# Unread unit-matrix matmuls in nine kinds ahead of the upward products, and half of the 512-token products as two halves

## The chip, the cores and the metric

The kernel runs on one core of one Trainium2 chip. The metric is the device time of one execution in microseconds (us), lower is better.

## The reference

Two transformer blocks of two layers each on 256 tokens of width 1024, in float32, and a context stream of 256 more tokens in the second block. Cut to the parts that carry the time:

```python
# first block, twice
mod = silu(c) @ w_ada[l] + b_ada[l]
h = rms_norm(x, g_pre_mix[l]) * (1 + sc_m) + sh_m
y = token_mixer(h, ...)                      # h @ w_in, two attentions, @ w_out
x = x + gt_m * rms_norm(y, g_post_mix[l])
h = rms_norm(x, g_pre_ffn[l]) * (1 + sc_f) + sh_f
y = (gelu(causal_conv3(h @ w_up_act)) * (h @ w_up_lin)) @ w_down     # 1024 -> 2816 -> 1024
x = x + gt_f * rms_norm(y, g_post_ffn[l])
# second block, on x and ctx; every FFN half is a SwiGLU 1024 -> 2816 -> 1024
s = s + 0.5 * gate * ((silu(h @ wg) * (h @ wu)) @ wd)
# layer 0: FFN half, convolution module (h @ w1, 31 taps, layer norm, @ w2), FFN half
# layer 1: FFN half, neighbourhood attention (h @ w_qkv, ..., @ w_o), FFN half on x alone
```

Only the x stream is returned.

## The kernel before, in words

A planner (`Plan`) writes out the whole program as one list of steps, and five classes, one per engine, walk that list and issue their own part of each step. Semaphores count finished work; `wait_ge` waits on such a count. So the order of the work on each engine is that of the list.

All weights come from DRAM in units of 128 x 1024 numbers, numbered in the order in which the planner takes them (`Plan.unit`). A ring of eight `raw` buffers receives them by SP's DMAs. ScalarE rounds a unit to fp32r (`upper`, line 1510, into `sh`), VectorE subtracts to get the remainder (`lower`, line 1806, into `sl`), in rings of six. Unit numbers also go to the modulation weights, which are not split and which VectorE alone multiplies (line 1820), between the others at planned rates. Activations are split in the same way into `hH` and `hL`, tokens along the columns: 256 for x alone, 512 with the context. A true product is then three fp32r matmuls that add in one PSUM bank, issued by `Tensor.mm3` at lines 1239 (high by high), 1240 (high weights by low activations in upward products) and 1241.

Upward products (step `prod`, method `Tensor.prod`) hold a 128 x 128 block of weights stationary and stream the tokens. One call works through one unit: eight blocks k, 24 matmuls, all of 256 or all of 512 columns, into one of eight PSUM banks. Its waits come first: that the bank is free, that the unit is split (`weights`), and ahead of each k that the activations are there (`act_ready`). Calls come from:

- `ffn1` (first block, each layer): 22 pairs of products of 256 tokens (`w_up_act`, `w_up_lin`), one stage of 44 calls each.
- `ffn2` on both streams (three times): the first three pairs go through `products`, in two passes of 256 tokens each over the same units (`begun` marks the second pass of each, which goes to the other half of the bank), so that the first can start before all tokens are normalized. Then 8 pairs of 512 tokens, the downward half, 11 pairs of 512 tokens, the downward half. Between the first products stand transposes (`turn`, line 1352) of the norm still under way.
- `ffn2` on x alone (the last): four pairs are made token by token, then 7 and 11 pairs of 256 tokens.
- `conv`: three pairs by `products`, five pairs of 512 tokens; the taps of the convolution (line 1447, plain f32) and the mean (line 1459) stand between them.
- `na`: eight products of 256 tokens for the queries, eight of 512 for the keys, with attention steps between.

Downward products (`down`) hold activations stationary and stream weights, 512 columns; they go through `mm3` as well.

Plain f32 work on TensorE is of other lines: transposes (1352, 1277, 1367, 1415: the data stationary, the unit matrix streamed, 128 columns), the attention's last matmul (1435, 64 columns), the taps (1447, 512 columns), and `warm` (line 1264), which issues matmuls of 256 columns with the unit matrix of the constants `C` as the stationary operand into a bank whose content nobody reads. `warm` stands ahead of stages at which TensorE would wait.

Of the kernel before, what the change touches and what calls it, by code (L numbers as in the profile page):

```python
# [16 lines left out]
KD = 8  # L17
# [33 lines left out]
for _n, _i, _w in VECS:  # L51
    VAT[(_n, _i)] = NV
    NV += _w

C_ID, C_0, C_CM, C_CS = 0, 128, 256, 384
NCST = 384 + 32

# [1165 lines left out]
class Tensor(Engine):  # L1223
# [79 lines left out]
    def prod(self, s):  # L1303
        cols = s["cols"]
        b = s["b"]
        if not s.get("begun"):
            self.wait_ge(self.gone(b))
        hi, lo = self.weights(s["unit"])
        H, L = self.m["hH"], self.m["hL"]
        w = cols.stop - cols.start  # L1310
        out = self.buf(b)[:, cols] if "begun" in s else self.buf(b)[:, 0:w]
        for k in range(KD):
            self.act_ready(s["act"], k, range(cols.start // 128, cols.stop // 128))
            c = slice(k * 128, (k + 1) * 128)
            x = self.mm3(out, hi[:, c], lo[:, c], H[:, k, cols], L[:, k, cols], k == 0, k == KD - 1)
        x.then_inc(self.sems["mm"], 1)
        if s["last"]:
            self.done("mm", ("full", b), ("w_used", s["unit"]), ("act_used", s["act"]))
        else:
            self.done("mm")  # L1320
# [1170 lines left out]
```

## Time and profile before

| what | us |
|---|---|
| median of the two runs shown | 2509.11 (2506.05 to 2512.16) |
| the profiled execution, its own time | 2495.19 |
| its span, first to last instruction | 2493.4 |
| PE (TensorE matmul) busy | 2411.0 of the span |
| PEld (TensorE weight load) busy | 2026.2 |
| DVE (VectorE) busy | 1677.2 |
| ACT (ScalarE) busy | 1082.1 |
| mean granted TensorE clock | 0.99 |

The profile is of one execution. Matmuls are pipelined: a duration of one is longer than the time to the start of the next, so what a stream of them costs is read from the starts, or from the length of a stretch over the matmuls in it. A granted clock of 1.00 is 2.4 GHz, 0.50 is 1.2 GHz. In a table of stretches the number in brackets counts every instruction that touches the stretch, so it can be one or two over the matmuls that start there.

### The profile page before, as it was taken

The page shows a single profiled execution, that of the slowest core. Times are in us where ns is not written, and L with a number is a line of the kernel's source. Part 1 is how long each engine was busy: PE and PEld are TensorE (multiplying, and loading weights), DVE is VectorE, ACT ScalarE, POOL GpSimd, SP SyncE. Part 2 cuts the span into 40 slices and gives each one's busy share as a digit, 9 for nine tenths or more (in the row PEclk, how much of TensorE's full clock was granted, in tenths as well). Part 3 has the DMA queues.
Part 4 walks back from the last instruction along what each step waited for, and adds up shares of the span by engine and source line. Part 5 has one row for each costly group of instructions (what it writes and reads, how often), then busy time and mean ns, then how long its engine had stood idle before and what let it go on. Part 6 is the DMA issues. An engine that isn't in the chain of part 4 may idle for free.

```text
span 2493.4 us, 34671 instructions
## 1 busy us (share of the span) xinstructions
PE 2411.0 (97%) x13076; PEld 2026.2 (81%) x13076; DVE 1677.2 (67%) x2620; ACT 1082.1 (43%) x1851; POOL 394.2 (16%) x431
## 2 busy tenths in 40 slices
PE   6999999989999999999979999999999999999998
PEld 5778987779988888887648888889888888777997
DVE  6967987769995776777965565565565556356554
ACT  4566545666554222237744322224322225344543
POOL 1111101101211101106840100100100110001101
PEclk9999999999999999999989999999999999999999
DMA  8656885557773454442202443442453443322562
GB/s 323 233 197 217 311 315 191 193 195 253 267 258 123 186 203 171 167 173 77 68 26 96 150 178 120 166 169 94 152 186 123 156 144 127 106 90 91 190 202 94
DMA packets 123335, 422.55 MB, mean 169 GB/s; under 512 B 15904, under 2 KB 20128, under 8 KB 123168
## 3 DMA queue, kind: packets, MB, share of 16 engines
q1 hardware_dynamic: 122608, 418.55, 48.1%
q8 instruction: 104, 1.70, 0.3%
q10 hardware_dynamic: 560, 1.79, 0.2%
q14 instruction: 63, 0.52, 0.1%
HBM read 419.17 MB, written 1.11 MB: 169 GB/s over the span
## 4 chain that ended last, share of the span: by engine, by line
PE 88%; DVE 6%; ACT 2%; issue 1%; POOL 1%; DMA 0%; DVEq 0%; ACTq 0%; POOLq 0%
PE ps L1239 27%; PE ps L1240 27%; PE ps L1241 27%; PE ps L1435 2%; PE ps L1447 2%; DVE sl L1806 1%; PE ps L1352 1%; DVE mjunk L1820 1%; PE ps L1415 1%; POOL ap L2335 1%; PE ps L1404 1%; ACT junk L1533 0%; DMA X<-in_x 0%; DVE sc L2021 0%; DVE hL L1895 0%
## 5 line engine op out<-in xcount | busy, mean ns | idle before, releaser
L1510 ACT ACTIVATE sh<-raw 128x1024 fp32r<-128x1024 f32 x534 | 552.2, 1043 | 898.8 <-PE ps L1241 898.3
L1239 PE MATMUL ps<-hH,sh 128*128 128x256 f32 (+1 forms) x2496 | 821.2, 329 | 1.6 <-DVE hL L1895 1.6
L1241 PE MATMUL ps<-hH,sl 128*128 128x256 f32 (+1 forms) x2496 | 816.5, 327 | 0.0
L1240 PE MATMUL ps<-hL,sh 128*128 128x256 f32 (+1 forms) x2496 | 816.5, 327 | 0.0
L1806 DVE TENSOR_TENSOR sl<-raw,sh 128x1024 fp32r<-128x1024 f32 x534 | 640.8, 1220 | 110.8 <-ACT sh L1510 110.2
L1820 DVE CUSTOM_DVE_ANT_0 mjunk<-raw,cB,V 128x1024 bf16<-128x1024 f32 x384 | 499.1, 1300 | 26.3 <-DMA C<-in_cst 8.6
L1239 PEld LDWEIGHTS ps<-hH,sh 128*128 128x128 f32 x2496 | 469.4, 188 | 52.9 <-issue 5.2
L1240 PEld LDWEIGHTS ps<-hL,sh 128*128 128x128 f32 x2496 | 468.7, 188 | 49.2 <-issue 1.7
L1241 PEld LDWEIGHTS ps<-hH,sl 128*128 128x128 f32 x2496 | 469.2, 188 | 48.1
L2308 POOL TENSOR_TENSOR uLl<-F,uHh 128x256 fp32r<-128x256 f32 (+1 forms) x132 | 170.8, 1294 | 1165.2 <-ACT uHh L1695 1043.0
L1241 PE MATMUL ps<-sh,uLl 128*128 128x512 f32 x792 | 311.8, 394 | 0.0
L1240 PE MATMUL ps<-sl,uHh 128*128 128x512 f32 x792 | 311.7, 394 | 0.0
L1239 PE MATMUL ps<-sh,uHh 128*128 128x512 f32 x792 | 310.5, 392 | 0.0
L2133 DVE TENSOR_TENSOR F<-S,ps 128x512 f32<-128x512 f32 (+1 forms) x88 | 54.6, 621 | 306.8 <-issue 283.7
L1239 PE MATMUL ps<-sh,hH 128*128 128x512 f32 (+2 forms) x512 | 204.5, 399 | 19.2 <-DVE hL L1895 9.7
L1240 PE MATMUL ps<-sl,hH 128*128 128x512 f32 (+2 forms) x512 | 197.2, 385 | 0.0
L1241 PE MATMUL ps<-sh,hL 128*128 128x512 f32 (+2 forms) x512 | 197.1, 385 | 0.0
L1239 PEld LDWEIGHTS ps<-sh,uHh 128*128 128x128 f32 x792 | 148.9, 188 | 33.8 <-DVE sl L1806 0.4
L1240 PEld LDWEIGHTS ps<-sl,uHh 128*128 128x128 f32 x792 | 149.0, 188 | 33.5
L1241 PEld LDWEIGHTS ps<-sh,uLl 128*128 128x128 f32 x792 | 149.0, 188 | 31.6
L1239 PEld LDWEIGHTS ps<-sh,hH 128*128 128x128 f32 x512 | 98.1, 192 | 41.9 <-issue 16.0
L1241 PEld LDWEIGHTS ps<-sh,hL 128*128 128x128 f32 x512 | 97.8, 191 | 19.7
(168 smaller groups left out, 2058.5 us busy)
## 6 DMA issues: line engine op xcount, KB each, us to landing
raw<-in_w SPq DMA_DIRECT2D x752, 512.0 KB, 4.6
G<-gates SPq DMA_DIRECT2D x14, 512.0 KB, 6.3
raw<-in_w SPq DMA_DIRECT2D x16, 256.0 KB, 4.6
cB<-in_rpb SPq DMA_DIRECT2D x64, 64.0 KB, 2.7
raw<-in_w SPq DMA_DIRECT2D x4, 492.0 KB, 6.1
S<-in_rows SPq DMA_DIRECT2D x6, 256.0 KB, 3.3
X<-in_x ACTq DMA_DIRECT2D x1, 1024.0 KB, 12.1
X<-in_ctx SPq DMA_DIRECT2D x1, 1024.0 KB, 5.8
```

The source lines that it names most:

```text
L1239: self.e.matmul(out, lh, rh, start=start, stop=False)
L1240: self.e.matmul(out, lh, rl, start=False, stop=False)
L1241: return self.e.matmul(out, ll, rh, start=False, stop=stop)
L1352: x = self.e.transpose(self.buf(p["b"])[:, k * 128:(k + 1) * 128], src[:, k * 128:(k + 1) * 128], ident)
L1404: x = self.e.matmul(ps[:, :], self.m["qT"][pr, c, i], self.m["kT"][pr, c, :], start=True, stop=True)
L1435: x = self.e.matmul(o[:, 64 * (hd % 8):64 * (hd % 8) + 64], p[:, (j * nb + c) * 128:(j * nb + c + 1) * 128], v, start=c == 0, stop=c == nb ...
L1447: x = self.e.matmul(ps[:, :], wd[:, k, :], up[:, :, k:k + 256], start=k == 0, stop=k == n - 1)
L1510: self.e.activation(self.m["sh"][k % SPL][:, 0:w], self.m["raw"][r % RAW][:, 0:w], ACT.Copy).then_inc(self.sems["w_hi"], 1)
L1806: self.e.tensor_tensor(lo[:, 0:w], raw[:, 0:w], hi[:, 0:w].bitcast(F32), ALU.subtract).then_inc(self.sems["w_lo"], 1)
L1820: self.e.tensor_tensor_reduce(out=self.m["mjunk"][:, :], in0=raw[:, 0:D], in1=self.m["cB"][:, st, :], scale=1.0, scalar=o, op0=ALU.mult, o ...
L2133: self.e.tensor_tensor(F[:, 0:N], self.buf(s["s"])[:, 0:N], self.buf(s["bu"])[:, s["o"]:s["o"] + N], ALU.mult).then_inc(self.sems["v_ps"], 1)
L2308: self.e.tensor_tensor(lo, self.buf(s["f"])[:, 0:N], hi.bitcast(F32), ALU.subtract).then_inc(self.sems["p_sb"], 1)
```

## The change

`Tensor.prod` gets a list of nine kinds, `NUDGES`, each a number of matmuls and a width. The kind is chosen by the weight unit, `unit // 2 % 9`. Ahead of the product's first true matmul so many matmuls with the unit matrix stationary and the first columns of the constants streamed are written into the same columns of the bank; the true product, which begins with `start=True`, overwrites them. In addition a product of 512 tokens whose unit number has `unit % 8 < 4` is made as two halves of 256 tokens, each through all eight k and each with its own unread matmuls. All other steps and their order stay.

```diff
--- before.py
+++ after.py
@@ -52,6 +52,7 @@
     VAT[(_n, _i)] = NV
     NV += _w
 
+NUDGES = ((0, 0), (1, 128), (2, 128), (1, 64), (1, 32), (1, 256), (2, 64), (1, 16), (1, 96))
 C_ID, C_0, C_CM, C_CS = 0, 128, 256, 384
 NCST = 384 + 32
 
@@ -1309,10 +1310,18 @@
         H, L = self.m["hH"], self.m["hL"]
         w = cols.stop - cols.start
         out = self.buf(b)[:, cols] if "begun" in s else self.buf(b)[:, 0:w]
-        for k in range(KD):
-            self.act_ready(s["act"], k, range(cols.start // 128, cols.stop // 128))
-            c = slice(k * 128, (k + 1) * 128)
-            x = self.mm3(out, hi[:, c], lo[:, c], H[:, k, cols], L[:, k, cols], k == 0, k == KD - 1)
+        halves = (slice(0, 256), slice(256, 512)) if w == 512 and s["unit"] % 8 < 4 else (slice(0, w),)
+        for half in halves:
+            n, wide = NUDGES[s["unit"] // 2 % len(NUDGES)]
+            part = slice(cols.start + half.start, cols.start + half.stop)
+            for k in range(KD):
+                self.act_ready(s["act"], k, range(part.start // 128, part.stop // 128))
+                if k == 0:
+                    for _ in range(n):
+                        self.e.matmul(out[:, half.start:half.start + wide], self.m["C"][:, C_ID:C_ID + 128],
+                                      self.m["C"][:, 0:wide], start=True, stop=True)
+                c = slice(k * 128, (k + 1) * 128)
+                x = self.mm3(out[:, half], hi[:, c], lo[:, c], H[:, k, part], L[:, k, part], k == 0, k == KD - 1)
         x.then_inc(self.sems["mm"], 1)
         if s["last"]:
             self.done("mm", ("full", b), ("w_used", s["unit"]), ("act_used", s["act"]))
```

## Rows read from the trace of the kernel before

**Rows 1.** The page: busy shares, and the chain that ended last by engine and line.
```profile
PE 2411.0 (97%) x13076; PEld 2026.2 (81%) x13076; DVE 1677.2 (67%) x2620; ACT 1082.1 (43%) x1851; POOL 394.2 (16%) x431
...
PE 88%; DVE 6%; ACT 2%; issue 1%; POOL 1%; DMA 0%; DVEq 0%; ACTq 0%; POOLq 0%
PE ps L1239 27%; PE ps L1240 27%; PE ps L1241 27%; PE ps L1435 2%; PE ps L1447 2%; DVE sl L1806 1%; PE ps L1352 1%; DVE mjunk L1820 1%; PE ps L1415 1%; POOL ap L2335 1%; PE ps L1404 1%; ACT junk L1533 0%; DMA X<-in_x 0%; DVE sc L2021 0%; DVE hL L1895 0%
```

**Rows 2.** Table of stretches, PE alone: start:end us, length, busy (matmuls), granted clock, DMA share, GB/s.
```profile
207.79:327.57 119.78, 119.78 (x1057) 1.00 0.83 294
559.65:679.44 119.79, 119.79 (x1057) 1.00 0.74 259
742.74:753.72 10.98, 10.98 (x100) 1.00 0.46 144
754.51:777.21 22.70, 22.70 (x196) 1.00 0.41 136
777.21:866.81 89.60, 89.60 (x387) 1.00 0.44 160
866.81:927.25 60.44, 60.44 (x266) 1.00 0.53 194
1116.30:1124.57 8.27, 8.27 (x76) 1.00 0.67 230
1125.36:1139.58 14.22, 14.22 (x124) 1.00 0.37 112
1378.40:1468.00 89.60, 89.60 (x386) 1.00 0.41 144
1468.00:1529.60 61.60, 61.60 (x266) 1.00 0.41 147
2327.28:2365.47 38.19, 38.19 (x339) 1.00 0.58 193
2395.69:2455.55 59.86, 59.86 (x529) 1.00 0.63 206
```

**Rows 3.** Timeline of PE: start us, duration us, engine, line, operation; behind the fourth upward product of an ffn2.
```profile
753.37 0.28 PE L1239 MATMUL ps<-hH,sh 128*128 128x256 f32 x1
753.49 0.28 PE L1240 MATMUL ps<-hL,sh 128*128 128x256 f32 x1
753.60 0.28 PE L1241 MATMUL ps<-hH,sl 128*128 128x256 f32 x1
753.72 1.03 PE L1352 MATMUL ps<-C,PT 128*128 128x128 f32 x8
754.51 0.36 PE L1239 MATMUL ps<-hH,sh 128*128 128x256 f32 x1
754.71 0.28 PE L1240 MATMUL ps<-hL,sh 128*128 128x256 f32 x1
754.83 0.28 PE L1241 MATMUL ps<-hH,sl 128*128 128x256 f32 x1
754.94 0.28 PE L1239 MATMUL ps<-hH,sh 128*128 128x256 f32 x1
755.06 0.28 PE L1240 MATMUL ps<-hL,sh 128*128 128x256 f32 x1
755.18 0.28 PE L1241 MATMUL ps<-hH,sl 128*128 128x256 f32 x1
```

**Rows 4.** Chain that ended last, in order of time: start us, us, group.
```profile
1186.57 5.16 PE ps L1447 x12
...
2168.60 0.84 PE ps L1435 x8
2295.32 0.87 PE ps L1352 x8
2296.20 6.05 PE ps L1264 x28
```

**Rows 5.** Timeline of PE around two transposes between downward matmuls of the second mixer.
```profile
504.23 0.39 PE L1241 MATMUL ps<-sh,hL 128*128 128x512 f32 x1
504.46 0.38 PE L1415 MATMUL ps<-C,S 128*128 128x128 f32 x2
504.60 0.48 PE L1239 MATMUL ps<-sh,hH 128*128 128x512 f32 x1
504.91 0.39 PE L1240 MATMUL ps<-sl,hH 128*128 128x512 f32 x1
505.14 0.40 PE L1241 MATMUL ps<-sh,hL 128*128 128x512 f32 x1
505.37 0.40 PE L1239 MATMUL ps<-sh,hH 128*128 128x512 f32 x1
```

**Rows 6.** Table of stretches, all engines: busy us (instructions) of PE, PEld, DVE, ACT, POOL.
```profile
207.80:327.60 119.80, 119.80 (x1057) 119.80 (x1058) 107.03 (x158) 70.56 (x109) 16.88 (x21) 1.00 0.83 295
777.20:866.80 89.60, 89.60 (x386) 72.20 (x385) 60.99 (x84) 27.55 (x37) 18.60 (x10) 1.00 0.44 160
1112.70:1157.40 44.70, 44.05 (x325) 39.05 (x324) 27.90 (x42) 30.77 (x53) 17.04 (x20) 1.00 0.34 107
```

## The prediction

> **What bounds the kernel now.** I began with the busy shares and the chain that ended last on the page: TensorE (PE) is busy 97% of the span and makes 88% of the chain, nearly all of it by lines 1239 to 1241, the three matmuls of `mm3` [rows 1]. Everything the change touches is issued by `Tensor.prod`, so the question is whether PE has any air in the product stages. The table of stages says no: in every one of its stretches PE's busy time is the length of the stretch [rows 2]. A busy PE alone doesn't say how fast it streams, so I took the pitch, start to start, as length over matmuls. The first up stage is 22 x 2 products x 24 matmuls of 256 tokens = 1056 in 119.78 us: 0.1134 us each. The second up stage and the last FFN (2 x 18 products, 336 and 528 matmuls in its two stretches) have the same pitch. But 192 matmuls of 256 tokens from 754.51 take 22.70 us: 0.1182. Two rhythms exist at the same granted clock (1.00 in all rows). Products of 512 tokens run at 89.60/384 = 0.2333 (from 777.21 and from 1378.40), the downward ones at 60.44/264 = 0.2289 or at 61.60/264 = 0.2333, same code, same widths [rows 2]. The rhythm is a matter of history: before the eight transposes at 753.72 matmuls start 0.11 apart, behind them 0.12 [rows 3]. The stretch from 1116.30 runs at 8.27/72 = 0.115, and behind eight more transposes the one from 1125.36 at 14.22/120 = 0.1185 [rows 2]. A rhythm then stays until something interrupts the stream.
>
> **What is added: unread matmuls.** Following the planner's unit numbers, there are 312 calls of `prod`, 180 of 256 tokens and 132 of 512. Of the 132, 70 have `unit % 8 < 4` and become two halves, each with its own unread matmuls. With `unit // 2 % 9` that makes 443 unread matmuls in 345 groups of one or two: 152 of 128 columns, 44 of 256, 135 of 64, and 112 of 96, 32 or 16. All are plain f32 with the unit matrix stationary, the form of `warm`. Prices from the chain: 28 of 256 columns take 6.05 us, 0.216 each; eight transposes of 128 columns 0.87, 0.109 each; eight of 64 columns 0.84, 0.105 each; twelve of 512 take 5.16, 0.430 each [rows 4]. From 256 up the price doubles with width, from 128 down it is flat: the weight load, one per matmul, sets it. How a group of two sits inside a product stream is shown once between downward matmuls: the first of two transposes starts at 504.46, the second true matmul behind them at 504.91; 0.45 less one normal pitch of 0.23 is 0.22 for two, 0.11 each, entry and exit included [rows 5]. So 44 x 0.216 = 9.5 us, and 399 x 0.11 = 43.9 us; sum 53.4. For a group of one, which the trace doesn't show, I add 5 ns for entry and exit: 345 x 0.005 = 1.7. Total 55 us. Bounds: the 112 of 96 columns and less are not in the trace. Were the weight load not their floor, the 64-column row halved, 0.053, would be the low end for them (-6 us); the high end is that a group of one pays the late start behind it, 0.31 where 0.23 is normal [rows 5], whole and on top of its 0.11: 247 groups x 0.08 = +20 us. The value I take is that of the nearest row, in which the late start is inside the 0.22.
>
> None of it has cover. The stretches are full of PE [rows 2], and PE is at the end of each product's chain: the next product's matmuls queue behind the unread ones, and ScalarE's `upper`, VectorE's `lower` and SP's weight loads wait for PE, not PE for them: in the first up stage, the tightest, VectorE is busy 107.03 of 119.80 us [rows 6]. Later weights make nothing late next. Only beside the taps (line 1447), in the conv stage's second pass, PE has 44.70 - 44.05 = 0.65 us of air [rows 6]; I take nothing off for it. No DMA moves, no queue is passed, no wait is added: the unread matmuls stand behind the same waits as before, and they write the columns that the product then overwrites.
>
> **What is changed: the halves.** A split product trades 24 matmuls at 0.2333 = 5.60 us for 48 of 256 tokens. At 0.1134 that is 5.44 (-0.16), at 0.1182 it is 5.67 (+0.07). Over 70 products: -11 to +5 us. Weight loads double there; in 256-token stages the load side is already busy 119.80 of 119.80 us while in 512-token stages it is 72.20 of 89.60 [rows 6]. So the halves give up the cover that a long matmul gives its load.
>
> The Trainium skill, TensorE: Matmul & The Clock Gate, section "Wait — 56ns, not 53.3ns?", has a fixed cost of about 2.5 ns per matmul at the full clock, by which 1680 more matmuls would cost 4.2 us in either rhythm. The trace doesn't agree in the fast one (twice 0.1134 is less than 0.2333) and about agrees in the slow one (0.2364, 3.1 ns more) [rows 2].
>
> **What moves: the rhythm.** Each group interrupts the stream and the rhythm is drawn anew. Of 17 stretches of 256-token products that begin behind f32 work in this trace, I count 11 slow and 6 fast; [rows 2] shows five of the fast and two of the slow. I take 0.65 slow. Of today's 4320 matmuls of 256 tokens some 3240 are fast: 0.65 x 3240 x 4.8 ns = +10.1 us; of the 1080 slow ones 0.35 x 1080 x 4.8 ns = -1.8; the split products at the same odds: 70 x (0.65 x 0.07 - 0.35 x 0.16) = -0.7. Unsplit 512-token products were at 0.2333 in every stretch, so nothing. Sum +8. Bounds: all fast -5 - 11 = -16 us; all slow +16 + 5, and downward work at 0.2333 throughout (some 3200 matmuls x 4.4 ns) 14 more: +35.
>
> **The sum** against the profiled execution: 2495.2 + 55 + 8 = 2558 us. The runs shown have a median of 2509.1, 13.9 above that execution. Were the two up stages and the last FFN slow in them, that is 2976 x 4.8 ns = 14.3 us, which would explain all of it and would not come on top; were it something else, it would: 2572. No row decides. I take the middle, 2565 us, 56 us or 2.2% above the median.
>
> **The rivals.**
> (a) The interruptions bring the fast rhythm nearly everywhere: 2495 + 55 - 16 = 2534, with the offset 2548; within 2%. For it: some stretches behind `warm` are fast (the two up stages, the last FFN) [rows 2], and the unread ones are of its form. Against: 11 of 17 went slow. The narrow ones at their low end would put it 6 us lower. 0.28.
> (b) Not slower than before: the interruption frees the pitch from what holds it above the columns' own time. 512 columns of plain f32 take 0.430, as two passes of 0.215, yet the fp32r matmul takes 0.2333 [rows 2, 4]. If every product began at 0.215 and 0.1075 and held it, 1488 unsplit matmuls of 512 tokens would give 1488 x 18 ns = 27 us, the split 1680 x 18 = 31, the 4320 of 256 tokens 28: 86 against 55, so about 2464 to 2478. It decides where the mean pitch of 512 falls under about 0.221. Against: no stretch behind any interruption went under 0.2289 or 0.1134 [rows 2]. 0.05.
> (c) Slow rhythm everywhere, downward stages too: 2495 + 55 + 35 = 2585. 0.12.
> (d) The unread f32 matmuls are dearer than the rows say. The Trainium skill, FP8 and Floating Point Precision, section TensorE Precision Notes, gives true FP32 four passes through the array. As a mechanism here, 256 columns would take four times 0.107 = 0.43 and 128 columns 0.21: 44 x 0.21 + 152 x 0.10 = 25 us more, 2591. By that rule the trace doesn't agree: 0.216 for 256 columns, with the clock at 1.00 [rows 2, 4]. 0.02.
>
> **How the numbers follow.** My forecast's case has 0.53, (a) 0.28, (b) 0.05, (c) 0.12, (d) 0.02. Two per cent of the median is 50 us (2459 and 2559), about what a measurement of this kernel can tell from no change. The forecast's case spans 2550 to 2582, with 0.07 of its 0.53 under 2559; (a) is within 2% whole, (b) but for 0.02; (c) and (d) are slower. Slower 0.60, within 2% 0.38, faster 0.02. Leaving (b) and the thin ends of (a), (c) and (d) out, the range is 2534 to 2590.
>
> **What would show it.** The first up stage would grow from 119.8 us by 48 unread matmuls, 6.3 us, to 126 if fast and at most 131 if slow; the first `ffn2` by 83, some 11 us. PE's busy time should stay the length of each such stretch. In groups by line a new line of plain f32 matmuls stands with 443, and 1680 more in lines 1239 to 1241 together. I am wrong if the 64-column ones and narrower fall clearly under 0.1 us each, if a group of one costs over 0.15, if products of 512 tokens leave 0.2333, or if PE shows idle time in a product stage.

## The result, and the profile after

The changed kernel takes 2605.8 us (two runs, 2605.55 and 2606.02) where the kernel before took 2509.1 (2506.05 and 2512.16): a ratio of 1.0395, interval 1.0369 to 1.0421, slower. Over the 45 runs of before that stand beside the experiments below its median is 2504 us (2496 to 2513), so the cost of the change is about 100 us. I had forecast 2565. The direction was right, the size was not, and the time lies above my range of 2534 to 2590.

Between the two profiled executions the span grows by 110.4 us (2493.4 to 2603.8). The page of the profile after, busy shares and the chain that ended last, to be read beside [rows 1]:

```profile
PE 2521.1 (97%) x15642; PEld 2211.4 (85%) x15642; DVE 1680.9 (65%) x2620; ACT 1081.4 (42%) x1851; POOL 378.4 (15%) x431
...
PE 89%; DVE 6%; ACT 2%; issue 1%; POOL 1%; DMA 0%; DVEq 0%; ACTq 0%; POOLq 0%
PE ps L1240 26%; PE ps L1242 26%; PE ps L1241 26%; PE ps L1321 4%; PE ps L1456 2%; PE ps L1444 2%; DVE sl L1815 1%; DVE mjunk L1829 1%; PE ps L1361 1%; PE ps L1424 1%; POOL ap L2344 1%; PE ps L1413 1%; ACT junk L1542 0%; DMA X<-in_x 0%; DVE sc L2030 0%
```

PE's busy time grows by 110.1 us, that is by all of the difference. PEld, whose weight loads run beside the matmuls, grows by 185 us, and none of the other engines by more than 4. (The lines of `mm3` are now 1240 to 1242; 1321 is the unread matmul.) The count of PE's matmuls grows by 2566, where 443 unread ones and 1680 for the halves would make 2123. The 443 too many are in this view, the groups of line 1321, one for each width:

```profile
L1321 PE MATMUL ps<-C 128*128 128x128 f32 x304 | 50.0, 274 | 1.0 <-DVE hL L1904 1.0
L1321 PE MATMUL ps<-C 128*128 128x64 f32 x270 | 40.1, 257 | 0.3 <-DVE hL L1904 0.3
L1321 PE MATMUL ps<-C 128*128 128x256 f32 x88 | 26.3, 380 | 0.0
L1321 PE MATMUL ps<-C 128*128 128x96 f32 x74 | 13.2, 260 | 0.0
L1321 PE MATMUL ps<-C 128*128 128x32 f32 x82 | 12.6, 235 | 0.0
L1321 PE MATMUL ps<-C 128*128 128x16 f32 x68 | 9.9, 221 | 0.0
```

These are 304 instructions of 128 columns where the code has 152 statements, 270 of 64 for 135, 88 of 256 for 44, and so on: 886 for 443. A plain f32 matmul in the code is two matmuls on TensorE, each with a weight load. The timeline of PE in the first up stage shows one such statement of 64 columns (start us, duration us, engine, line, operation), listed as x2:

```profile
210.71 0.28 PE L1241 MATMUL ps<-hL,sh 128*128 128x256 f32 x1
210.82 0.28 PE L1242 MATMUL ps<-hH,sl 128*128 128x256 f32 x1
210.94 0.33 PE L1321 MATMUL ps<-C 128*128 128x64 f32 x2
211.08 0.36 PE L1240 MATMUL ps<-hH,sh 128*128 128x256 f32 x1
211.28 0.28 PE L1241 MATMUL ps<-hL,sh 128*128 128x256 f32 x1
...
211.64 0.28 PE L1241 MATMUL ps<-hL,sh 128*128 128x256 f32 x1
211.76 0.28 PE L1242 MATMUL ps<-hH,sl 128*128 128x256 f32 x1
211.87 0.28 PE L1240 MATMUL ps<-hH,sh 128*128 128x256 f32 x1
211.98 0.28 PE L1241 MATMUL ps<-hL,sh 128*128 128x256 f32 x1
...
212.21 0.28 PE L1240 MATMUL ps<-hH,sh 128*128 128x256 f32 x1
212.32 0.28 PE L1241 MATMUL ps<-hL,sh 128*128 128x256 f32 x1
```

From the unread start at 210.94 to the second true start at 211.28 are 0.34 us, less one normal pitch of 0.12: 0.22 for one statement, where I had 0.11. Taken so over all 345 groups of this trace, from the starts of the single instructions, a statement of 16 to 128 columns costs 0.225 us and one of 256 costs 0.432: 399 x 0.225 + 44 x 0.432 = 109 us. That is the difference of the spans. The same timeline also shows the rhythm change: starts 0.12 apart before and for the first matmuls behind, 0.11 from 211.76 on.

The stretches (start:end us, length, busy (matmuls), granted clock, DMA share, GB/s) below answer to 207.79 and 559.65 of [rows 2], to this one of the kernel before, a stage of 22 products of 512 tokens, and to 866.81 of [rows 2]:

```profile
927.25:1050.45 123.20, 123.20 (x530) 1.00 0.49 178
```

```profile
208.24:341.92 133.68, 133.68 (x1152) 1.00 0.75 266
575.24:709.19 133.95, 133.95 (x1156) 1.00 0.69 240
967.67:1101.09 133.42, 133.42 (x896) 1.00 0.47 170
906.06:967.67 61.61, 61.61 (x267) 1.00 0.52 188
```

The first up stage goes from 119.8 to 133.7 us, where I had 126 to 131. PE has no idle time in any of them and the clock is at 1.00, so there was indeed no cover.

### The profile page after: what moved, and what is told of

Same layout as the page of the kernel before. It is cut to its first block, busy times and chain, and to the rows that moved or that the text cites. A ratio compares the mean times of both kernels' runs of the same rounds, so it can differ in the third digit from the quotient of the medians.

```text
span 2603.8 us, 39803 instructions
## 1 busy us (share of the span) xinstructions
PE 2521.1 (97%) x15642; PEld 2211.4 (85%) x15642; DVE 1680.9 (65%) x2620; ACT 1081.4 (42%) x1851; POOL 378.4 (15%) x431
## 4 chain that ended last, share of the span: by engine, by line
PE 89%; DVE 6%; ACT 2%; issue 1%; POOL 1%; DMA 0%; DVEq 0%; ACTq 0%; POOLq 0%
PE ps L1240 26%; PE ps L1242 26%; PE ps L1241 26%; PE ps L1321 4%; PE ps L1456 2%; PE ps L1444 2%; DVE sl L1815 1%; DVE mjunk L1829 1%; PE ps L1361 1%; PE ps L1424 1%; POOL ap L2344 1%; PE ps L1413 1%; ACT junk L1542 0%; DMA X<-in_x 0%; DVE sc L2030 0%
## 5 line engine op out<-in xcount | busy, mean ns | idle before, releaser
L1240 PE MATMUL ps<-hH,sh 128*128 128x256 f32 (+1 forms) x3056 | 942.9, 309 | 0.0
L1242 PE MATMUL ps<-hH,sl 128*128 128x256 f32 (+1 forms) x3056 | 908.7, 297 | 0.0
L1241 PE MATMUL ps<-hL,sh 128*128 128x256 f32 (+1 forms) x3056 | 908.4, 297 | 0.0
L1241 PEld LDWEIGHTS ps<-hL,sh 128*128 128x128 f32 x3056 | 576.5, 189 | 21.4 <-issue 0.2
L1242 PEld LDWEIGHTS ps<-hH,sl 128*128 128x128 f32 x3056 | 575.4, 188 | 22.6
L1240 PEld LDWEIGHTS ps<-hH,sh 128*128 128x128 f32 x3056 | 575.8, 188 | 21.4 <-issue 0.2
L2317 POOL TENSOR_TENSOR uLl<-F,uHh 128x256 fp32r<-128x256 f32 (+1 forms) x132 | 156.1, 1183 | 1274.5 <-ACT uHh L1704 1147.2
L1321 PE MATMUL ps<-C 128*128 128x128 f32 (+5 forms) x886 | 152.0, 271 | 1.3 <-DVE hL L1904 1.3
L1321 PEld LDWEIGHTS ps<-C 128*128 128x128 f32 x886 | 131.6, 190 | 10.7 <-issue 5.7
```

What stands on the lines that cost most here:

```text
L1240: self.e.matmul(out, lh, rh, start=start, stop=False)
L1241: self.e.matmul(out, lh, rl, start=False, stop=False)
L1242: return self.e.matmul(out, ll, rh, start=False, stop=stop)
L1321: self.e.matmul(out[:, half.start:half.start + wide], self.m["C"][:, C_ID:C_ID + 128], self.m["C"][:, 0:wide], start=True, stop=True)
L2317: self.e.tensor_tensor(lo, self.buf(s["f"])[:, 0:N], hi.bitcast(F32), ALU.subtract).then_inc(self.sems["p_sb"], 1)
```

## The experiments

Each kernel is measured against the kernel before, run on the same chip. I call a product of 256 tokens fast or slow by the median distance of its matmuls' starts, which is close to 0.113 or to 0.118 us in every one of them. All such counts are of one profiled execution of each kernel. Four theories stood at the start. *Two instructions*: the surplus over my forecast is the second instruction of each plain f32 matmul. *Rhythm*: it is the slow rhythm. *Doubled loads*: it is the halves. And, for the 13.9 us between the first profile of before and its two timed runs, that the up stages fall now into one rhythm, now into the other.

**The kernel before, again.** No edit.

> The kernel before, unchanged, once more with a profile. Its first profiled execution was at 2495.2 us, the two timed runs at 2506 and 2512. Theory rhythm-of-before: the time of before differs from run to run because the up stages and the last FFN fall into the slow rhythm (0.118 us a matmul) or the fast one (0.113); then the spread is in steps of about 5 us (each up stage) and 4 us (the last FFN), and a profile at 2500 or more shows one of these stretches at 124.8 instead of 119.8 us. Rival: the offset lies elsewhere (weights arriving late, the start); then the up stages stay at 119.8 us in a slow run too.

Measured: 2504.1 us, 2496.1 to 2511.3 in ten runs. This time the profiled execution has a span of 2500.7 us, and the table of stretches (columns as above) shows one stretch in the other rhythm:

```profile
209.34:329.12 119.78, 119.78 (x1057) 1.00 0.83 294
561.95:681.91 119.96, 119.96 (x1059) 1.00 0.74 258
2332.70:2372.36 39.66, 39.66 (x339) 1.00 0.56 187
2403.16:2463.02 59.86, 59.86 (x530) 1.00 0.64 205
```

Both up stages are fast again, against the theory, but the last FFN's first upward stretch takes 39.66 us for 336 matmuls (0.118) where it took 38.19 in [rows 2]. So the same program runs in different rhythms in different executions. That is 1.5 of the 7.3 us by which this span is longer. Start by start, the two traces of the same 13076 matmuls differ by 1.7 us in the products of 256 tokens, by 1.9 in the downward matmuls of 512 columns (most of it in two stages that run at 0.2333 instead of 0.2289), by 1.3 in 24 matmuls near the start, and by 2.3 in PE's other work. So the upward rhythm is one part of the spread of before and not all of it.

**The unread matmuls without the halves.**

```diff
-        halves = (slice(0, 256), slice(256, 512)) if w == 512 and s["unit"] % 8 < 4 else (slice(0, w),)
+        halves = (slice(0, w),)
```

> The unread matmuls alone, no halves: 354 statements, 36 of them of 256 columns. Theory two-instructions: a plain f32 matmul statement is two TensorE instructions with a weight load each, so a statement costs 0.225 us up to 128 columns and 0.43 at 256: 318 x 0.225 + 36 x 0.43 = 87 us above before, of which the profile shows 708 matmuls of that line. Rival (one instruction at 0.11 us, the rest a slower rhythm): 354 matmuls, about 40 us plus up to 16 us of slow rhythm.

Measured: 2587.5 us, ratio 1.0325 (1.0308 to 1.0343), 83 us above before. The group of the unread line in its trace, against 354 statements in the code:

```profile
L1321 PE MATMUL ps<-C 128*128 128x128 f32 (+5 forms) x708 | 122.4, 271 | 1.3 <-DVE hL L1904 1.3
```

Two instructions hold, and the price of 87 to within the spread of before. "One instruction" would have given 40 to 56. Trace to trace, the upward products with the unread matmuls among them take 1331.1 us against 1244.9 in the first trace of before, 86 more.

**The halves without the unread matmuls.**

```diff
-            n, wide = NUDGES[s["unit"] // 2 % len(NUDGES)]
+            n, wide = 0, 0
```

> The halves alone, no unread matmuls. Theory two-instructions: the halves are worth -11 us if their stretches run at 0.1134 us a matmul and +5 us if at 0.118; they have nothing to do with the 97 us. Since nothing interrupts the stream between products, each stretch should keep the rhythm it starts with. Rival (doubled weight loads are dear): 1680 more loads cost 20 us or more, the time is 2520 or above.

Measured: 2490.8 us, ratio 0.9938 (0.9921 to 0.9956): 13.7 us faster than before. So doubled loads are not dear, but the 13.7 is more than the halves account for. Its table of stretches:

```profile
209.53:334.09 124.56, 124.56 (x1058) 1.00 0.81 285
567.63:687.51 119.88, 119.88 (x1058) 1.00 0.75 259
762.58:873.61 111.03, 111.03 (x769) 1.00 0.44 156
934.03:1055.34 121.31, 121.31 (x817) 1.00 0.49 180
```

The first up stage ran slow here (124.56 for the same 1056 matmuls as 119.88 behind it), the 5 us step that I had supposed. The last row is the stage of 22 products that took 123.20 whole; with 12 of them as halves it takes 121.31. Counted product by product, all halves in it run at 0.1134. Over all upward products this trace has 1240.4 us and the first trace of before 1244.9, so 4.5 us less, and some 9 less but for the slow first up stage; the rest of the 13.7 is a difference between executions that these traces do not place. The changed kernel has 1349.5 us for the same products and its 443 unread statements, 109.1 more than the halves alone: the price of the unread ones, whole.

**One transpose for each unread matmul.** A transpose of the unit matrix is one instruction, also plain f32 and 128 columns.

```diff
-                        self.e.matmul(out[:, half.start:half.start + wide], self.m["C"][:, C_ID:C_ID + 128],
-                                      self.m["C"][:, 0:wide], start=True, stop=True)
+                        self.e.transpose(out[:, half.start:half.start + 128], self.m["C"][:, C_ID:C_ID + 128],
+                                         self.m["C"][:, C_ID:C_ID + 128])
```

> The changed kernel with each unread matmul made as a transpose of the unit matrix (128 columns) instead of a plain f32 matmul, so one instruction instead of two, same places, same number of statements (443). Theory two-instructions: 443 x 0.109 = 48 us of unread work where the changed kernel has 110, so about 2545 to 2550 us. Rival (the price is that of interrupting the stream and of the rhythm behind it, not of the instructions): it stays near 2600.

Measured: 2556.2 us, ratio 1.0200 (1.0185 to 1.0215). Half of the added time is gone with half of the instructions; groups of one cost 0.11 us by the starts, 50 us for 443. The interruptions are the same in number and place, so they are not what the other half was paid for. The time is 6 us over what I expected; 168 of the 320 products of 256 tokens are slow here, for 117 in the changed kernel, and 51 x 24 x 4.8 ns are 6 us.

**Two transposes for each.** The loop over `n` runs to `2 * n`; the rest as above.

> The changed kernel with each unread statement made as two transposes of the unit matrix: as many TensorE instructions (886) as the changed kernel's 443 plain f32 statements issue. Theory two-instructions (the price goes by instructions, 0.11 us each, for its weight load): 886 x 0.11 = 97 us, about 2600 us, as the changed kernel but for its 44 wide ones (9 us less: 2595 to 2603). Rival (a plain f32 matmul is dear for its arithmetic, not for its number): about as with one transpose, 2556 to 2570.

Measured: 2602.6 us, ratio 1.0395 (1.0378 to 1.0413), beside 1.0395 for the changed kernel. With as many instructions the time is back, although no arithmetic of the old form is left: up to 128 columns the price is per instruction. That the two ratios are equal to the last digit is luck, and each stands against other runs of before. By the starts the unread ones are 11 us cheaper here, since the 44 wide statements of the changed kernel cost 0.432 each, and this execution has 153 slow products for 117 (4 us) and slower downward stages (3 us). The rows have shortest, median and longest duration in ns:

```profile
L1321 PEld LDWEIGHTS ps<-C x886: 137/140/199, 209.1 to 2560.1; 128*128 128x128 f32 x178
L1321 PE MATMUL ps<-C x886: 269/272/327, 209.3 to 2560.2; 128*128 128x128 f32 x178
```

**Kinds of one width: 16 columns, and 64.** Both without halves, one statement ahead of each of the 312 products. In the trace of the changed kernel the rhythm behind an unread matmul had not looked like a coin toss: between products of 256 tokens it was fast behind 25 of 25 of width 32 and 26 of 26 of width 16, slow behind 27 of 31 single ones of width 64. It does not go by width alone: behind 96 columns 24 of 24 were fast, behind single ones of 128 only 3 of 31.

```diff
-            n, wide = NUDGES[s["unit"] // 2 % len(NUDGES)]
+            n, wide = 1, 16          # 1, 64 in the other
```

> One unread matmul of 16 columns ahead of each of the 312 products, no halves. Theory two-instructions: 312 x 0.225 = 70 us. Theory width-picks-rhythm: behind this kind nearly all products of 256 tokens run at 0.1134, so against the fast profile of before 70 - 5 = 65: about 2560 to 2565 us. Rival (rhythm drawn at random): as e8_all_64.

> One unread matmul of 64 columns ahead of each of the 312 products, no halves; the same number and the same price of unread matmuls as with 16 columns, 70 us. Theory width-picks-rhythm: behind this kind nearly all products of 256 tokens run at 0.118, 180 x 24 x 4.8 ns = 21 us more than with 16 columns: about 2580 to 2585 us. Rival (rhythm drawn at random): within 5 us of e7_all_16.

Measured: 2564.9 us (ratio 1.0231, 1.0211 to 1.0250) and 2576.6 us (1.0280, 1.0255 to 1.0304). The first number is as expected; the second is 12 us above it, not 21. The first up stage of each, 16 columns first, then 64, for the same number of instructions:

```profile
208.33:338.92 130.59, 130.59 (x1145) 1.00 0.78 273
571.89:702.49 130.60, 130.60 (x1145) 1.00 0.70 244
```

```profile
209.53:342.64 133.11, 133.11 (x1145) 1.00 0.75 268
574.75:707.87 133.12, 133.12 (x1145) 1.00 0.70 242
```

Behind 16 columns between two products of 256 tokens, 158 of 158 products are fast. Behind 64 columns 109 of 158 are slow, 103 more slow products in all than with 16 columns, which at 24 x 4.8 ns each makes the 12 us. They come in a fixed pattern: in both up stages and in the last FFN one product is fast and the next two slow, over and over. An independent draw does not do that; the rhythm follows from what interrupts and from what went before, which one of the two rhythms alone does not describe, since a slow product is followed now by a slow one, now by a fast one.

**All products of 512 tokens as halves, nothing unread.** The condition `s["unit"] % 8 < 4` falls.

> No unread matmuls, all 132 products of 512 tokens as halves. With half of them the time was 13.7 us below before. Theory rhythm: a long product of 512 columns is what brings the 256-column stream back to 0.1134 us a matmul; without any, the stretches that start slow stay slow to their end (768 matmuls at 0.118 in the first upward stage of each two-stream FFN, which is 1.2 us dearer than whole products), and only the stretches that start fast gain (22 products x 0.16 = 3.5 us each). So little or nothing is added to the gain of the 70: 2485 to 2500. Rival (each half is cheaper by itself): 132/70 of the gain, 2478.

Measured: 2503.1 us, ratio 1.0001 (0.9985 to 1.0018), with the wide spread of before (2498.7 to 2512.1). It is 3 us over the range that I expected. All of the gain of the 70 halves is lost by making 132. Its stretches, the 24 products that took 112.3 us in before (22.70 + 89.60 in [rows 2]) and two stages of 22:

```profile
762.04:875.19 113.15, 113.15 (x963) 1.00 0.43 155
936.79:1056.49 119.70, 119.70 (x1057) 1.00 0.50 182
1538.06:1662.43 124.37, 124.37 (x1057) 1.00 0.45 161
```

A stretch without long products keeps the rhythm that it starts with, 0.118 in the first and the third.

**All halves in unbroken runs, and ten unread matmuls.** 114 of the 132 products as halves; one statement of 32 columns ahead of the second product of each run of six or more, ten in the kernel. `run` and `reset` are set by a walk over the plan's steps.

```diff
-        halves = (slice(0, 256), slice(256, 512)) if w == 512 and s["unit"] % 8 < 4 else (slice(0, w),)
+        halves = (slice(0, 256), slice(256, 512)) if w == 512 and s["run"] >= 6 else (slice(0, w),)
...
-            n, wide = NUDGES[s["unit"] // 2 % len(NUDGES)]
+            n, wide = (1, 32) if s["reset"] and half.start == 0 else (0, 0)
```

> All products of 512 tokens in unbroken runs of six or more products as halves (114 of 132), and one unread matmul of 32 columns ahead of the second product of each such run, ten in all, 2.2 us. Theory rhythm: that kind of interruption inside a 256-column stream leaves it at 0.1134 (it did 25 times of 25 in the changed kernel), so all ten runs go fast and stay: 114 x 0.157 = 18 us, the 24 slow products of 256 tokens 2.8 us, slow draws of before 9 us on average, less 2.2: 2475 to 2480 us, with less spread between runs than before. Rival (the rhythm is a draw): the gain is that of the halves alone less 2 us, about 2490, and some of the ten runs stand at 0.118.

Measured: 2480.4 us, ratio 0.9894 (0.9875 to 0.9913), 2478.6 to 2481.2 in four runs. It beats both kernels: 23 us under before, 125 under the changed one. That is 1.1%, and clear of the spread. Its stretches, in the order of those above with the first up stage ahead:

```profile
209.26:329.36 120.10, 120.05 (x1058) 1.00 0.84 293
756.62:865.86 109.24, 109.24 (x965) 1.00 0.44 159
926.28:1046.23 119.95, 119.95 (x1059) 1.00 0.50 182
1523.08:1643.03 119.95, 119.95 (x1059) 1.00 0.47 167
```

All ten runs stand at 0.1134 to 0.114. The timeline of PE at the unread pair of the second of these stretches shows the starts 0.12 apart ahead of it; the stretch takes 109.24 us, where without the pair (the kernel after this one) it takes 113.15.

```profile
759.42 0.28 PE L1252 MATMUL ps<-hL,sh 128*128 128x256 f32 x1
759.54 0.28 PE L1253 MATMUL ps<-hH,sl 128*128 128x256 f32 x1
759.66 0.30 PE L1332 MATMUL ps<-C 128*128 128x32 f32 x2
759.80 0.36 PE L1251 MATMUL ps<-hH,sh 128*128 128x256 f32 x1
760.00 0.29 PE L1252 MATMUL ps<-hL,sh 128*128 128x256 f32 x1
```

**The same without the ten, and the ten without the halves.** `(1, 32)` becomes `(0, 0)` in the one; `halves` is always `(slice(0, w),)` in the other.

> e6_reset without its ten unread matmuls: 114 products as halves, nothing unread. Theory rhythm: the three first upward stages of the two-stream FFNs start at 0.118 and stay there, and in other stages it is chance; the time goes back to about 2500 us with a spread of 10 us, 20 us above e6_reset although it issues less. Rival (the gain of e6_reset is that of the shorter halves): it is 2 us faster than e6_reset, 2478.

> The ten unread matmuls alone, all products of 512 tokens whole. Theory rhythm: the ten runs of 256-token products go at 0.1134 in every execution, the 24 slow products in front of the 512-token ones included: 2.8 us gained and 2.2 paid against the fast profile of before, and the slow draws of the up stages (9 us in the median) gone: 2494 to 2497 us with a spread under 4 us, where before has 2496 to 2513. Rival (the spread of before comes from elsewhere): median 2504 and the same spread.

Measured: 2499.8 us for the halves alone (ratio 0.9994, 0.9976 to 1.0011; 2494.0 to 2513.6) and 2495.5 us for the ten alone (0.9973, 0.9961 to 0.9984; 2492.8 to 2497.9). The ten together with the halves are worth 23 us, the ten alone 8, and the halves alone nothing that can be told from zero (by the interval 6 us at most). Trace to trace, the upward products with the ten take 1226.7 us, without the ten 1246.4: 19.7 us, and the spans differ by 19.6. Of 408 products of 256 tokens 23 are slow with the ten and 229 without. In the table of the halves alone the missing time stands where the theory puts it:

```profile
757.37:870.52 113.15, 113.15 (x962) 1.00 0.43 156
932.12:1051.82 119.70, 119.70 (x1057) 1.00 0.50 183
1530.82:1655.19 124.37, 124.37 (x1057) 1.00 0.45 160
```

And the spread falls: to 5 us in ten runs with the ten alone (I had said under 4), where before had 13 in 19 runs on that chip and the halves alone 20 in ten; with the ten and the halves to 3 in four runs, where before had 17 in 13. So much of the spread hangs on the rhythm that the ten set, though the two traces of before show that it is not all.

## Why the prediction was right or wrong

**What bounds the kernel, and that nothing covers the additions: right.** PE's busy time is the length of each stretch before and after, and the span grows by what PE's busy time grows.

**What is added: the step that failed.** I counted 443 statements and priced each at the time of one row of the trace, 0.11 or 0.216 us. The rows count instructions, and a plain f32 matmul is two. The term "44 x 0.216 + 399 x 0.11 + 1.7 = 55 us" measures 109; my high end for it, +20, did not reach there either. My own sign fired: a group of one costs 0.225 us, and I had said that over 0.15 I would be wrong. The kernel before had what was needed: [rows 4] has 28 matmuls of line 1264 where the code calls `warm(14)`, and twelve of line 1447 where the code has six taps. I read durations off those rows and never held their counts against the code. My nearest row for a group, two transposes in [rows 5], was of the only plain f32 form that is one instruction per statement.

**Rival (d)** had the right price for 256 and 128 columns, and I gave it 0.02. Its 2591 is still too low, because it left the narrower ones at 0.11. The Trainium skill, FP8 and Floating Point Precision, section TensorE Precision Notes, gives true FP32 four passes. By that rule the trace agrees, once the statement is what is priced: 0.432 us for 256 columns is 4 x 0.107, as two instructions of 0.216. My sentence that the trace doesn't agree compared one of the two instructions with the rule for both. For 64 columns and fewer the rule falls short: the four passes of 64 would be half of those of 128, and 0.225 us stays 0.225. In the trace of the kernel with 16 columns the starts of the two weight loads, too, stand 0.11 us apart, so a load that can't be had faster would explain the floor; no run separates the load from other fixed costs of an instruction.

**The width is flat from 128 down: right,** and now shown to 16 columns; what I bounded for the narrow ones from below did not come.

**Rivals (a) to (c).** In no stretch did the pitch fall under 0.1134 or 0.2289 behind an interruption, so (b) found nothing to rest on; the rhythm went neither fast nor slow everywhere in the changed kernel, so neither (a) nor (c) was its case. (a) is what the ten placed interruptions do.

**The halves: right by the traces.** -11 to +5 us was the range. By the medians they gave -13.7 alone, outside it; by the traces the upward products gave -4.5, and some -9 but for an up stage without any halves that happened to be slow. The fixed cost of 2.5 ns per matmul of the Trainium skill (TensorE: Matmul & The Clock Gate, section "Wait — 56ns, not 53.3ns?") is not what decides here: 1680 more matmuls came out cheaper, not 4.2 us dearer.

**The rhythm: right that it exists and that interruptions change it, wrong that it is a draw.** My +8 us came out near nothing in the changed kernel: counted product by product, 203 of its 320 calls' worth of 256-token products are fast (63%; I had 35%), so 203 x 2.72 + 117 x 2.84 us = 884 for what before took 135 x 2.72 + 45 x 2.84 + 70 x 5.60 = 887. My odds came from stretches behind other f32 work, most of it transposes, and did not carry over to these interruptions.

**The offset of 13.9 us: half right.** Up stages do fall into the slow rhythm in some executions (124.56 for 119.88 with the halves alone), but in both traces of before both were fast, so that they make the 13.9 is not shown; and two timed runs were too few: the median of before is 2504, and the changed kernel's profile and runs agree with each other, so the difference of the profiles, 110, overstates the cost by what a fast execution of before saves.

## What to carry to other kernels

Hold the counts of the rows against the statements of the code before a duration is multiplied: a row prices an instruction, and one statement may be two. On PE a plain f32 matmul of 128 columns or fewer cost two instructions of 0.11 us each however narrow it was, so a filler that has to be short should be a transpose, or be few. And where one program's time varies by some 0.7% from run to run, compare the lengths of equal stretches between its executions; here one short interruption at the right place fixed the pitch of a thousand matmuls behind it, while 443 of them cost about 100 us, four times the 23 that ten placed ones brought together with the halves.

## What the runs showed of the hardware that I had not expected

A steady stream of weight load and matmul pairs of 256 fp32r columns has two stable pitches, 0.1134 and 0.118 us, at the same granted clock of 1.00, and keeps the one it is in for over a thousand matmuls (119.78 and 124.56 us for 1056). In the traces without unread matmuls no product of 256 tokens that directly followed another had the other pitch. Which one follows an interruption depends on its form and on what went before: behind a plain f32 matmul of 16 columns inside such a stream it was the fast one 158 times of 158, behind one of 64 columns the slow one 109 times of 158, in a cycle of three products. A product of 512-column matmuls between those of 256 also brings the fast one back: in the run with 70 halves the half behind a whole product of 512 columns, with nothing between, was fast 23 times of 23; with 132 halves and no long product left whole stages stayed slow. Upward products of 512 columns ran at 0.2333 in all of their undisturbed stretches, that is dearer per column than two fast halves at 0.2268. What inside TensorE makes two pitches, and why the same program starts a stage in one or the other from execution to execution, the runs do not tell; I only saw them through the starts of the matmuls.
